# 64 prompt tokens moved from the first output and query pass to the second, in a one-core hybrid decoder step

## The reference, cut to what matters

```python
h = layer_norm(ALPHA * x + mix @ w_out, ln1_g, ln1_b)
y = layer_norm(ALPHA * h + peer_ffn(h, peer_w_query, peer_sub_keys, peer_u, peer_v), ln2_g, ln2_b)

def compress(rows, pe, w1, w2):            # the chunks: past keys (kv 0) and values (kv 1)
    blk = rows[:, idx] + pe                 # idx: 32 rows every 16
    return jnp.einsum('bnge,ef->bngf', gelu(jnp.einsum('bnlgd,lde->bnge', blk, w1)), w2)

def block(xc):                              # peer_ffn, for 128 tokens
    q = (xc @ w_query).reshape(128, 8, 2, 128)
    s = einsum('thcd,ckd->thck', q, sub_keys)
    top_s, top_i = lax.top_k(s, 16)
    cand_s = top_s[:, :, 0, :, None] + top_s[:, :, 1, None, :]
    cand_i = top_i[:, :, 0, :, None] * 128 + top_i[:, :, 1, None, :]
    best_s, best_j = lax.top_k(cand_s, 16)
    experts, gate = cand_i[best_j], softmax(best_s)
    act = gelu(einsum('thkd,td->thk', u_tab[experts], xc))
    return einsum('thk,thkd->td', gate * act, v_tab[experts])
```

## Time and profile before

| | us |
|---|---|
| three runs: median (lowest to highest) | 2564.53 (2562.35 to 2565.36) |
| the profiled execution | 2565.83 |
| its span, first to last instruction | 2564.0 |
| first u gather issued, first v gather issued | 753.4, 851.8 |
| last v gather issued | 2537.2 |
| granted TensorE clock, mean | 0.809 of 2.4 GHz |

### The profile page before, as it was taken

The page is one execution under the profiler, slowest core; times in us unless marked ns, Lnnn a source line. Parts: engine busy times, 40 slices in busy tenths (PEclk is TensorE's granted clock), DMA queues, the critical chain, the costliest instruction groups (busy, mean ns, idle before and its releaser), DMA issues.

```text
span 2564.0 us, 29141 instructions
## 1 busy us (share of the span) xinstructions
PE 1894.7 (74%) x9494; PEld 1079.4 (42%) x9494; DVE 1248.9 (49%) x2349; ACT 335.7 (13%) x787; POOL 719.3 (28%) x594
## 2 busy tenths in 40 slices
PE   8999999979999877757776663665563545988336
PEld 5777766544478654534554310221120002655000
DVE  0510122253048867677887535434433345477860
ACT  0000111422031000201100101101110010011011
...
DMA  9889979896349999999999999999999999999998
GB/s 397 301 344 358 371 274 379 340 374 257 121 184 361 395 409 409 408 411 412 409 409 410 410 397 410 410 397 392 416 385 397 421 421 422 421 421 414 417 420 342
DMA packets 213687, 964.23 MB, mean 376 GB/s; under 512 B 23937, under 2 KB 89474, under 8 KB 122818
## 3 DMA queue, kind: packets, MB, share of 16 engines
...
HBM read 955.81 MB, written 14.88 MB: 379 GB/s over the span
## 4 chain that ended last, share of the span: by engine, by line
DMA 47%; PE 34%; DVE 8%; issue 4%; SPq 2%; ACTq 2%; POOL 1%; ACT 1%; POOLq 0%; DVEq 0%
DMA sb<-in_peer_u,sb 20%; DMA sb<-in_peer_v,sb 19%; PE bank L1038 14%; PE bank L1344 4%; DMA sb<-in_nsa_t 4%; DVE sb L2319 4%; PE bank L1386 4%; DMA sb<-in_nsa_v 3%; PE bank L1677 2%; PE bank L1102 2%; PE bank L1142 2%; POOL sb L2427 1%; ACTq L892 1%; DMA sb<-in_a_v 1%; SPq L613 1%
## 5 line engine op out<-in xcount | busy, mean ns | idle before, releaser
L1677 PE MATMUL bank<-sb 128*32 128x512 f32 x2304 | 475.8, 846 | 528.6 <-DMA sb<-in_peer_v,sb 509.7
L2319 DVE CUSTOM_DVE_ANT_1 sb<-sb 128x2048 f32<-128x2048 f32 x224 | 513.4, 2293 | 517.6 <-DMA sb<-in_peer_u,sb 515.3
L2427 POOL DMA_INDIRECT sb<-in_peer_v,sb x288 | 407.1, 1413 | 444.3 <-PE bank L1677 346.8
L2427 POOL DMA_INDIRECT sb<-in_peer_u,sb x288 | 304.1, 1056 | 763.5 <-DVE sb L2319 531.2
L1677 PEld LDWEIGHTS bank<-sb 128*32 128x32 f32 x2304 | 62.3, 124 | 750.1 <-DMA sb<-in_peer_v,sb 711.3
L1038 PE MATMUL bank<-sb 128*128 128x288 f32 x1408 | 351.6, 409 | 11.8 <-DMA sb<-in_w_in 11.8
L1038 PEld LDWEIGHTS bank<-sb 128*128 128x128 f32 x1408 | 266.8, 191 | 95.5 <-issue 12.2
L1429 PE MATMUL bank<-sb 128*128 128x256 f32 x1024 | 292.1, 440 | 0.8 <-ACT sb L837 0.5
L1429 PEld LDWEIGHTS bank<-sb 128*128 128x128 f32 x1024 | 250.5, 309 | 76.6 <-issue 57.9
L2319 DVE CUSTOM_DVE_ANT_0 sb<-sb 128x2048 f32<-128x2048 f32 x64 | 146.4, 2292 | 78.4 <-DMA sb<-in_peer_u,sb 74.5
L1004 ACT ACTIVATE sb<-sb 128x32 f32<-128x32 f32 x288 | 83.1, 313 | 508.0 <-PE bank L1677 301.2
...
...
## 6 DMA issues: line engine op xcount, KB each, us to landing
sb<-in_a_k SPq DMA_DIRECT2D x128, 512.0 KB, 6.9
sb<-in_a_v SPq DMA_DIRECT2D x128, 512.0 KB, 6.8
...
sb<-in_nsa_t SPq DMA_DIRECT2D x200, 128.0 KB, 10.0
sb<-in_nsa_t ACTq DMA_DIRECT2D x184, 128.0 KB, 14.1
sb<-in_nsa_v SPq DMA_DIRECT2D x64, 128.0 KB, 15.9
```

The source lines that it names most:

```text
L1677: mm = pe.matmul(bank[g % 2][32 * c:32 * c + 32, :], diag[j % 4], rows[:, 512 * c:512 * c + 512], start=(s in FIRST), stop=(s in LAST), sk ...
L2319: dve.tensor_tensor_reduce(out=u, in0=u, in1=replica(g), scale=1.0, scalar=0.0, op0=ALU.mult, op1=ALU.add, accum_out=act16[:, r % 2, j:j + ...
L2427: pool.indirect_dma_start(rows[j % 4], None, dram[table], bass.IndirectOffsetOnAxis(ap=idx, axis=0)).then_inc(full[j % 4], 16)
```

## The change

The first pass takes 192 prompt tokens, in tiles of 128 and 64. The other 64 prompt tokens go with the 32 samples, a second pass of 96 rows among the slots: groups 6, 7 (prompt) and 8 (samples), where groups 6 and 7 take turns by four slots as 0 and 1 do. Chunks are compressed in two pieces every 2 slots from slot 15, keys and values without a break (before: three pieces every 3 slots, from 20 and from 72). What hangs on them comes earlier: block choice at 55 (82), sparse attention at 82 and 116 (123 and 157), output at 156 (198), queries at 180 (230), now a whole block of w_query per slot. v rows are taken 19 slots behind u rows, before 22. In the first pass a matmul of the 64-token tile writes 64 partitions of the bank; even and odd input slices go to the lower and upper half, and DVE adds both halves. In the second pass 96 rows are three quarters of a bank, each summed over all 16 input slices, and the fold is gone. Norm gains and tokens are loaded for 96 rows instead of 32, and the second norm's gains when all queries are done. Lines that are not shown adapt sizes, storage, counts of semaphores and the numbers at which choices and folds are made.

```diff
+GROUPS_1 = 6
+ROWS_1 = NSMP * (GROUPS_1 - 4)
+TOK_1 = P + ROWS_1
+ROWS_2 = T - TOK_1
+ROWS_P = NPROMPT - TOK_1
+PARTS_1 = P // ROWS_1
+
+
+def place(g):
+
+    if g < 4:
+        return 0, slice(32 * g, 32 * g + 32)
+    tile, row = (1, 32 * (g - 4)) if g < GROUPS_1 else (2, 32 * (g - GROUPS_1))
+    return tile, slice(row, row + 32)
...
-LAG = 22
+LAG = 19
 SLOTS_ALL = 32 * NGRP
 
 
-TAPS_AT = (20, 72)
-TAPS = {TAPS_AT[kv] + 3 * i + piece: (kv, i, piece) for kv in range(2) for i in range(2 * NB) for piece in range(3)}
+TAPS_AT = 15
+
+
+def taps_tick(kv, i):
+
+    n = 2 * NB * kv + i
+    return TAPS_AT + 2 * n
+
+
+TAPS = {taps_tick(kv, i) + piece: (kv, i, piece) for kv in range(2) for i in range(2 * NB) for piece in range(2)}
...
-PICK_AT = 82
-NSA_AT = (123, 157)
+PICK_AT = 55
+NSA_AT = (82, 116)
...
-OUT_AT = 198
-QUERY_AT = 230
-REPLICATE = {32 * (g - 1) + 20 + 2 * q: (g, q) for g in range(2, NGRP) for q in range(4)}
-
-
-SHARED = 64
+OUT_AT = 156
+QUERY_AT = 180
+REPLICATE = {32 * (g - 1) + 20 + 2 * q: (g, q) for g in range(2, NGRP) if g != 7 for q in range(4)}
+REPLICATE.update({192 + q: (7, q) for q in range(4)})
+
+
+def shared(s):
+
+    return s // 64 in (0, 3)
...
-    return (s // 4) % 2 if s < SHARED else s // 32
+    return 2 * (s // 64) + (s // 4) % 2 if shared(s) else s // 32
...
-CHOSEN_BY = {0: 1, 8: 2, 16: 3, 32: 4, 48: 5, 64: 6, 96: 7, 128: 8, 160: 9, 192: 10, 224: 11, 256: 12, 264: 13, 272: 14, 280: 15}
+CHOSEN_BY = {0: 1, 8: 2, 16: 3, 32: 4, 48: 5, 64: 6, 96: 7, 128: 8, 160: 9, 192: 10, 200: 11, 208: 12, 224: 13, 240: 14, 256: 15}
...
-        rows_of = [P, P, NSMP]
+        rows_of = [slice(0, P), slice(P - ROWS_1, P), slice(0, ROWS_2)]
...
-                    sp.dma_start(h_nat[0:NSMP, 2, :], dram["tokens"][NPROMPT:T]).then_inc(smp_tok_in, 16)
+                    sp.dma_start(h_nat[0:ROWS_2, 2, :], dram["tokens"][TOK_1:T]).then_inc(smp_tok_in, 16)
                     for n in range(2):
-                        sp.dma_start(smp_norm[0:NSMP, n, :], dram["norms"][n:n + 1, :].to_broadcast([NSMP, DM])).then_inc(smp_norm_in, 16)
+                        sp.dma_start(smp_norm[0:ROWS_2, n, :], dram["norms"][n:n + 1, :].to_broadcast([ROWS_2, DM])).then_inc(smp_norm_in, 16)
...
-                if i == 8:
-                    sp.wait_ge(folded_out, 4)
-                    for n in range(2):
-                        sp.dma_start(norm_2[:, n, :], dram["norms"][2 + n:3 + n, :].to_broadcast([P, DM])).then_inc(norm2_in, 16)
...
+                parts, rows = (1, P) if tt == 0 else (PARTS_1, ROWS_1)
                 for kt in range(4):
-                    mm = pe.matmul(bank[3 * (n % 2) + tt][:, :], mix(4 * kq + kt)[:, P * tt:P * tt + P], w[:, kt, :],
-                                   start=(kq == 0 and kt == 0), stop=(kq == 3 and kt == 3))
+                    own = slice(rows * (kt % parts), rows * (kt % parts) + rows)
+                    mm = pe.matmul(bank[3 * (n % 2) + tt][own, :], mix(4 * kq + kt)[:, P * tt:P * tt + rows], w[:, kt, :],
+                                   start=(kq == 0 and kt < parts), stop=(kq == 3 and kt >= 4 - parts))
...
-                query_rows(m, 0, NPROMPT).then_inc(item_used, 1)
+                query_rows(m, 0, TOK_1).then_inc(item_used, 1)
...
-                for l in range(6 * piece, min(16, 6 * piece + 6)):
+                for l in range(8 * piece, 8 * piece + 8):
...
-                    mm = pe.matmul(bank[2 + n][32 * kt:32 * kt + 32, :], smp_mix_t[:, 4 * kq + kt, :], w[:, kt, :],
-                                   start=(kq == 0), stop=(kq == 3))
+                    at = 4 * kq + kt
+                    first, last = kq == 0 and kt == 0, kq == 3 and kt == 3
+                    for own in range(0, ROWS_2, 32):
+                        rows = mix_2[:, at, own:own + 32] if own < ROWS_P else smp_mix_t[:, at, :]
+                        mm = pe.matmul(bank[2 + n][own:own + 32, :], rows, w[:, kt, :], start=first, stop=last, skip_group_check=True)
...
+            def query_of(m):
+                w = later_arrived(("wq", m))
+                if m == 0:
+                    pe.wait_ge(h_t_in, 12)
+                if m >= 2:
+                    pe.wait_ge(q_in, 18 + m - 1)
...
+                    mm = pe.matmul(bank[2 + m % 2][:, 0:ROWS_2], w[:, P * kt:P * kt + P], h_t2[:, kt, :], start=(kt == 0), stop=(kt == KT - 1))
+                mm.then_inc(later_used, 1)
...
-                if 0 <= d < 32:
-                    query_of(d // 2, d % 2)
-                if d >= 5 and d % 2 == 1 and d < 37:
-                    score_of((d - 5) // 2)
+                if 0 <= d < 16:
+                    query_of(d)
+                if 2 <= d < 18:
+                    score_of(d - 2)
...
+            FIRST_GROUPS = {0: (0, 1), 1: (), 2: (6, 7)}
...
-            def sample_row(n):
+            def second_rows(n):
                 if n == 0:
                     dve.wait_ge(smp_tok_in, 16)
-                dve.wait_ge(folded_out, n + 1)
-                hh = h_nat[0:NSMP, 2, 512 * n:512 * n + 512]
-                ch.tell(dve.scalar_tensor_tensor(out=hh, in0=hh, scalar=ALPHA, in1=bank[6 + n % 2][0:NSMP, :], op0=ALU.mult, op1=ALU.add,
-                                                 accum_out=ln[0:NSMP, 28 + n:29 + n]), wo_evac, 8 + n + 1)
+                dve.wait_ge(later_used, later_items.used["wo", 4 * n + 3])
+                hh = h_nat[0:ROWS_2, 2, 512 * n:512 * n + 512]
+                ch.tell(dve.scalar_tensor_tensor(out=hh, in0=hh, scalar=ALPHA, in1=bank[2 + n][0:ROWS_2, :], op0=ALU.mult, op1=ALU.add,
+                                                 accum_out=ln[0:ROWS_2, 28 + n:29 + n]), wo_evac, 8 + n + 1)
```

391 lines of the change are left out of this document (199 added, 192 removed).

## The result

The changed kernel takes 2579.0 us (median of four runs, 2574.2 to 2580.4) where the kernel before takes 2565.0 beside it (2562.4 to 2566.2): 1.0053 times as long, interval 1.0035 to 1.0070. It is **slower by 0.5%**, where 2544 us had been forecast. The profiled execution is the fastest of the four, 2574.2 us with a span of 2572.4.

The account below looks back on a forecast made before the run. PE's path was taken to bound the kernel before 753 us, mainly transfers behind it. Terms -21.7 - 7 + 3.8 + 3 + 1 = -20.9 us against the profiled 2565.8 gave 2544.9, adjusted to the median 2544 us; range 2526 to 2566.

Parts of the forecast that it names:

- Part 1: First output pass: paired 64-column matmuls shorten it to some 87 us; first gather comes 21.7 us earlier.
- the switches: First output pass: changes of matmul width, twice in each block, 0.32 us there and back, 3.8 us over 12 blocks.
- Rival A: First output pass: 64-column matmuls don't run side by side, so a block stays at 6.88 us; 2569 us, chance 0.08.
- Part 4: Chunk stage: chunks every 2 slots tighten the two buffers, PE waits 1 or 2 us at many; cost 3 us (0 to 16).
- Rival C: Chunk stage: the chunk buffers bind, costing 16 us in place of 3; 2557 us, chance 0.07.
- slower: Whole kernel: measurably slower than before, through Rival B in both stages or Rival A with Rival C; chance 0.08.
- sign of being wrong: GB/s between 860 and 1300 us falling under 400, or the output pass staying at 110 us.
- Part 2: Query pass and first slots: faster query blocks and more transfers there save 7 us of DMA time (2 to 9.6).
- Parts 3 and 5: Part 3: more bytes for tokens and norm gains, 3.8 us more; Part 5: late output, query and choice work, 1 us more.
- three times: Load of norm gains: if 96 partitions behave like 32, three times the bytes cost up to 13 us more.
- goes: Load of norm gains: if 96 partitions behave like 128, the transfer dip goes and 3 us come back.
- Rival B: Behind slot 156, PE at 1.2 GHz becomes the bound: 2567 us, 2588 if the output stage is slow too; chance 0.12.

## Why the prediction was wrong

**Part 1 was right.** 64-column matmuls run in pairs, the pass took 87.0 us where "some 87 us" stood, and the switches cost 4.3 us (114.38 less 16 x 6.88) against 3.8. Rival A is out. That the first gather came 22.0 us earlier for 21.7 is in part luck: the pass itself began 2.0 us earlier (614.79 for 616.75), and that start lies anywhere from 611.1 to 616.9 us in the profiled executions, with and without the change. From the start of the pass to the first gather it is 116.7 us for 136.6, 20.0 less.

**Part 4 is the step that failed**, in its term of 3 us, for which the runs show more than 20: 21 us of lost DMA time in the stage, 23 less with a chunk's taps in one slot, 29 less with the third buffer. It saw the right place ("the two chunk buffers are tighter", 15 us of room), and then went wrong twice. It set 14.0 us for ACT's pages and 2 for their issue against 15 of room; but the 14.0 stands from issue to landing, and from the buffer's release to the chunk's start it was 16.6 on average, and PE waited 3 to 7 us at every second chunk, not 1 or 2 at many. And it said "it costs only if the gathers in flight run out". This holds for a single halt (PE's 21 us at the weights cost 3), not for one that comes back with every chunk: then PE is never ahead, v gathers wait for PE 206 us of 380, and few are in flight. Their landing time shows it, 21.4 us before, in the changed kernel and with the third buffer from 1100 to 1240 us:

```profile
sb<-in_peer_v,sb POOLq DMA_INDIRECT x21, 10.0
```
```profile
sb<-in_peer_v,sb POOLq DMA_INDIRECT x22, 20.2
```

By number and landing time some 3 gathers are in flight in the changed kernel (an estimate: 41 u and v gathers in 140 us, 9.5 us each), 7 before. The cover named was an effect of the state that the edit ends. Rival C named the mechanism, priced it at 16 us and gave it 0.07; "slower" had 0.08, but for a slow clock or for A with C, not for C alone. The sign of being wrong that it named came: 384 GB/s from 860 to 1240 us.

**Part 2 was wrong by its 7 us and 2 more.** The first slots lose 13.9 us in 119, and lost 11.8 in 99. The faster query pass uses up its weights by 810 us, and until the chunks and value rows are under way the DMA engines have too little to do. The first v gather was forecast near 812 us and came at 823.1: in POOL's order a u gather stands before it, which waited 7.5 us for DVE. Two stretches of the changed kernel:

```profile
790.00:810.00 20.00, 20.00 (x123) 19.12 (x122) 18.83 (x42) 2.64 (x9) 5.12 (x4) 1.00 0.91 335
810.00:830.00 20.00, 17.43 (x82) 16.45 (x81) 14.88 (x41) 4.05 (x11) 11.23 (x6) 1.00 0.77 285
```

DVE (the third of the busy times) is full until 810, so u gathers can't come faster. The first stretch is no loss of the change, since before 813 to 833 us ran at 335 GB/s too; the second is. The shorter lag is worth 7 us with three buffers, but at a halt further on that the change itself brings in; in the kernel before it costs 5.

**Parts 3 and 5 were near.** 3 us for the bytes. The dip of the earlier trace rows is still there: the tokens and norm gains for 96 rows are issued at 1724 to 1725 us, and behind that stands

```profile
1730.00:1740.00 10.00, 1.94 (x8) 0.20 (x8) 1.11 (x1) 0.32 (x1) 3.74 (x4) 0.50 1.02 336
1740.00:1750.00 10.00, 2.55 (x10) 0.49 (x10) 1.19 (x2) 0.32 (x1) 1.71 (x2) 0.50 1.01 273
```

With the next 10 us (387) that is 6 us lost against some 4 before, so neither "three times" nor "goes"; and three times the dip of 262 GB/s would have been 8 us more by its own row, not the 13 of the prediction. From 2050 to 2200 us 4.6 us are lost, 3 more than in the like stretch of before, where 1 was taken and 4 was the other end.

**Rival B did not come**: behind slot 156 (PE begins its output blocks at 1767 us) the clock was 0.67 to 0.83 in stretches of 50 us up to 2050 us, and the rate 414 in the first of them, from 1750 to 1800, and 421 in the others. The clock's fall came elsewhere, in the narrow query passes.

With the third buffer the kernel comes to 12 us under the one before by the medians and to 16 by the two profiled spans (2547.9 and 2564.0), where the forecast had 21. In these spans the chunk stage loses what it lost before (16.5 us in 386 for 16.9) and so do the first slots (11.9 for 11.8): what is missing is part 2's 7 us, and part 4's 3 are not spent.
